# Attention through three ring banks, rotary embedding by copies, silu and the feature split moved in a two-layer hybrid mixer on one core

## The chip, the cores and the metric

The kernel runs on one core of one Trainium2 chip. The metric is the device time of one execution in microseconds (us), lower is better. Arrays are float32; most matrix products are written as three products of float32 halves (high and low parts).

## What is computed

Two layers (`DEPTH = 2`) over 1024 latent and 128 context tokens, 1152 in all, with 1024 features. Each layer normalises the tokens, modulates them, projects them through one combined weight, runs three branches (a gated linear recurrence A, differential attention B, a Fourier mixing C), multiplies each by its own silu gate, projects and merges them under sigmoid gates, and adds an output projection to the residual. For attention, cut to what matters here:

```python
q_b = rms_norm(qb.reshape(B, T, H_B, 2, DH_B), qn_g)      # 4 heads, 2 maps, 64 features
k_b = rms_norm(kb.reshape(B, T, H_B, 2, DH_B), kn_g)
q_b = axial_rope(q_b, rope)                               # latent tokens only: pairs (x1, x2) 16 apart
k_all = concat([axial_rope(k_b, rope), cached context keys])
w = softmax(q1 k1) - lam * softmax(q2 k2)                 # one 128-query block at a time
y_b = rms_norm(w @ v_all, sub_g) * (1 - lam_init) * silu(zb)
```

## The kernel before

Each weight block of 128 output channels is one `project`: three tiles of 384 tokens, each tile 8 x 3 products (high x high, low x high, high x low) into one PSUM bank; `take` hands out banks 0 to 2 in turn, and the reader frees a bank. SyncE loads the blocks in the order of `weight_order` two ahead, GpSimd splits each into high and low parts (L712, L714), TensorE multiplies (L358). The order of the instructions of every engine is written out by hand; semaphores tie them.

In a layer come first the recurrence heads, then `attention(l, h)` for four heads, then the Fourier groups, the merge of the three branches (two products for each of eight feature blocks: a gate G and a branch product Y) and the output projection O. Attention goes over nine positions, `BLOCKS = (0, CTX, 1, ..., 7)`: query blocks of 128, the context block second. At each position and for each of two maps m TensorE forms scores in banks 3 to 5 (L542, L543), VectorE takes the maximum (L1603), ScalarE the exponential (L1048). VectorE forms the weights (L1609 to L1614); TensorE turns them in groups of three 128x128 blocks (`transposed`, L555) through a ring of two banks, 6 and 7, ScalarE copies them (L1055), and TensorE multiplies them with the values (L568), whose result ScalarE reads from the same ring (L1066, L1068).

Between these steps stand projection tiles of the next head (`FIRST_GAP`, one at each position, and `SECOND_GAP`), of q, k, v and of the gate z, in this order: first scores, tile, two groups of turns of the position before, second scores, the third group, a second tile, values of the position before. The preparation of the next head lies there too: `head_sums` (L498) for the norm of q and k, `normed` on VectorE, and the rotary turn, which TensorE does as a product with a constant matrix (`rotated`, L506) whose result VectorE multiplies and adds (`turned`, L1571, L1574). The high and low parts (`high_parts` on ScalarE, `low_parts` on VectorE, L1581 to L1585) are made at the last position. `values_turned` (L515) turns the next head's values at the end of a head, in tile banks; for head 0 it stands behind the first scores. `output_sums`, `output_rstd` and `output_silu` finish the head before at positions 0 and 1; silu needs two table loads.

At the end of a layer ScalarE copies the merged features X to `h_hi` and VectorE forms `h_lo` (L1767) after the last branch product; ScalarE also issues eight loads of the residual, `x_res` (L1264), into the space of the branch features. The residual is added when an output block is ready:

```python
for j in range(KD):
    dve.wait_ge(o_xin, l * 16 * KD + 16 * KD)   # all eight x_res copies
    for t in range(NT):
        ...                                     # X = ps * gate + x_res, frees the tile's bank
```

At the start ScalarE issues the loads of the modulation weights (`ada_group`, 8 of 1 MB), the features X (8 of 576 KB) and the masks; SyncE starts on the weight blocks when the last X has landed. The first layer's features are squared, summed, scaled and modulated feature block by feature block (L1293, L1355, L776, L1359).

Of the kernel before, what the change touches and what calls it, by code (L numbers as in the profile page):

```python
# [19 lines left out]
F32 = mybir.dt.float32  # L20
# [27 lines left out]
IDENT, ONES, HEAD_ONES, ROT = range(4)  # L48
# [22 lines left out]
def weight_order():  # L71
# [3 lines left out]
    qkv = lambda h: [(("B", h, j), False, 20 + 3 * h + j) for j in range(3)]  # L75
    order += [a_block(0, j) for j in range(4)]
# [25 lines left out]
FIRST_GAP = (("q", 0), ("q", 2), ("k", 1), ("k", 2), ("v", 0), ("v", 1), ("v", 2), ("z", 0), ("z", 1))  # L102
SECOND_GAP = {0: ("q", 1), 1: ("k", 0), 8: ("z", 2)}
RING = 34


def mixer_kernel(nc, x_in, w_full, w_half, ada_first, ada_late, cond_rows, params, squares, masks, rope, dft_t, dft_c,
# [12 lines left out]
    off_m = off_c + 4 * 512 + (MASKS + 1) * P  # L120
# [14 lines left out]
    sq_c = at("sq_c", [P, 4, P], F32, off_c)  # L135
    mask = at("mask", [P, MASKS + 1, P], U8, off_c + 4 * 512)
# [17 lines left out]
    ident, ones, head_ones, rot_m = (sq_c[:, i, :] for i in range(4))  # L154
# [90 lines left out]
    with ctx:  # L245
        ps = ctx.enter_context(nc.psum_tensor("ps", [P, 8, 512], F32))

        def sem(name):
# [24 lines left out]
        b_raw_s, b_rs_s, b_qn_s, b_qk, b_vt_s, b_vtok, b_cache_k, b_cache_v, b_kv_out, b_hi, b_lo = (  # L273
            sem(n) for n in ("b_squares", "b_rstd", "b_normed", "b_qk",
                             "b_vt", "b_vtok", "b_cache_k", "b_cache_v", "b_kv_out", "b_hi", "b_lo"))
# [33 lines left out]
        seats = {}  # L309

# [35 lines left out]
        def _(pe):  # L346
            def take(*key):

                bank, nth = len(seats) % NT, len(seats) // NT
                seats[key] = bank, nth + 1  # L350
                if nth:
                    pe.wait_ge(tile_free[bank], nth)
                return bank

# [7 lines left out]
            def tile(l, name, t, kt=KD, hi=h_hi, lo=h_lo):  # L362

                n = place[l, name]
                if t == 0:
                    pe.wait_ge(w_split, n + 2)
                bank = take(l, name, t)
# [60 lines left out]
            def recurrence(l, h):  # L428
                a = l * HEADS + h
                last = h + 1 == HEADS  # L430
                for i, (kind, lev, g) in enumerate(units):
# [49 lines left out]
                    if g == 2:  # L481
# [3 lines left out]
                        if last and point == "ub":  # L485
                            head_sums(l, 0, 1)
                            rotated(l, 0, 0)
                        for name, t in a_gap(h, point):
                            tile(l, name, t)
                        if last and point == "ub":  # L490
                            rotated(l, 0, 1)

            def head_sums(l, h, m):

                for t in range(NT):
                    pe.wait_ge(b_raw_s, (l * HEADS + h) * 6 + (3 * m + t + 1))
                    bank = take(l, "sum", h, m, t)
                    pe.matmul(ps[:, bank, 0:TILE], head_ones, (b_kt if m else b_qt)[:, cols_of(t)],  # L498
                              start=True, stop=True).then_inc(tile_done[bank], 1)

            def rotated(l, h, m):

                pe.wait_ge(b_qn_s, (l * HEADS + h) * 2 + (m + 1))
                for i in range(2):
                    bank = take(l, "rot", h, m, i)
                    pe.matmul(ps[:, bank, :], rot_m, (b_kn if m else b_qn)[:, i * 512:(i + 1) * 512],  # L506
                              start=True, stop=True).then_inc(tile_done[bank], 1)

            def values_turned(l, h):

                pe.wait_ge(b_vt_s, l * HEADS + h + 1)
                for g in range(3):
                    bank = take(l, "vt", h, g)
# [3 lines left out]
                    mm.then_inc(tile_done[bank], 1)  # L517

            def output_sums(l, h):

                for t in range(NT):
                    if t == 0:
                        pe.wait_ge(b_os_s, (l * HEADS + h) * CH + CH)
                    bank = take(l, "osum", h, t)
                    pe.matmul(ps[:, bank, 0:TILE], ones, b_os[:, cols_of(t)],
                              start=True, stop=True).then_inc(tile_done[bank], 1)

            def attention(l, h):
                a = l * HEADS + h
                ring = a * RING  # L530
# [15 lines left out]
                def transposed(pos, g):  # L546
                    nonlocal ring
                    i = BLOCKS[pos]
                    if g == 0:
                        pe.wait_ge(b_w, a * CH + (pos + 1))  # L550
                    if ring > 1:
                        pe.wait_ge(b_ev, ring - 1)
                    for c in range(1 if i == CTX else 3):
                        kt = 3 * g + c
                        mm = pe.transpose(ps[:, 6 + ring % 2, c * P:(c + 1) * P],  # L555
                                          b_e0[pos % 2][:, kt * P:(kt + 1) * P], ident)
                    mm.then_inc(b_tr, 1)
                    ring += 1

                def values(pos):  # L560
                    nonlocal ring
                    i = BLOCKS[pos]
                    if pos == 0:
                        pe.wait_ge(b_vtok, a * 3 + 3)
                        pe.wait_ge(b_cache_v, 16 * a + 16)
                    pe.wait_ge(b_ev, ring)
                    for kt in range(1 if i == CTX else CH):
                        mm = pe.matmul(ps[:, 6 + ring % 2, 0:P], b_v[:, CH if i == CTX else kt, :], b_wt[:, kt, :],  # L568
                                       start=(kt == 0), stop=(kt == CH - 1 or i == CTX))
                    mm.then_inc(b_tr, 1)  # L570
                    ring += 1

                for pos in range(CH):
                    before = 0 if pos == 0 else 1 if BLOCKS[pos - 1] == CTX else 3
# [1335 lines left out]
```

## Time and profile before

| what | value |
|---|---|
| median of three runs | 3163.32 us (3162.22 to 3165.91) |
| the profiled execution's own time | 3163.95 us |
| its span, first to last instruction | 3161.9 us |
| TensorE products busy | 3043.5 us, 96% of the span |
| VectorE, ScalarE, GpSimd busy | 1440.4, 1069.6, 698.7 us |
| mean granted TensorE clock | 0.986 of 2.4 GHz |

The span is 2.05 us shorter than the execution's time. Products overlap in their records: a product of 384 columns is shown with 334 ns, but the next one starts 173 ns after it. An idle gap shown in brackets is the time since the record before ended, which is some 0.16 us after its last column was taken in.

### The profile page before, as it was taken

The page shows a single profiled execution, that of the slowest core. Times are in us where ns is not written, and L with a number is a line of the kernel's source. Part 1 is how long each engine was busy: PE and PEld are TensorE (multiplying, and loading weights), DVE is VectorE, ACT ScalarE, POOL GpSimd, SP SyncE. Part 2 cuts the span into 40 slices and gives each one's busy share as a digit, 9 for nine tenths or more (in the row PEclk, how much of TensorE's full clock was granted, in tenths as well). Part 3 has the DMA queues.
Part 4 walks back from the last instruction along what each step waited for, and adds up shares of the span by engine and source line. Part 5 has one row for each costly group of instructions (what it writes and reads, how often), then busy time and mean ns, then how long its engine had stood idle before and what let it go on. Part 6 is the DMA issues. An engine that isn't in the chain of part 4 may idle for free.

```text
span 3161.9 us, 43735 instructions
## 1 busy us (share of the span) xinstructions
PE 3043.5 (96%) x18336; PEld 2941.6 (93%) x18336; DVE 1440.4 (46%) x1920; ACT 1069.6 (34%) x2036; POOL 698.7 (22%) x404
## 2 busy tenths in 40 slices
PE   7999999999999999999979999999999999999999
PEld 3999988898899999999969999888988999999999
DVE  4655674666542102266247655655655420112331
ACT  5244345656542101111043334456555430101010
POOL 1211111111111233333322111111111122333332
PEclk9999999999999999999999999999999999999999
DMA  5111111000011112154211011100000101212232
GB/s 208 39 31 38 38 49 33 24 23 30 31 71 32 34 42 76 44 160 160 85 44 34 31 38 39 45 31 32 24 30 29 71 28 41 71 47 77 74 111 73
DMA packets 54675, 175.23 MB, mean 55 GB/s; under 512 B 5968, under 2 KB 13136, under 8 KB 52688
## 3 DMA queue, kind: packets, MB, share of 16 engines
q1 hardware_dynamic: 28800, 92.29, 9.6%
q10 hardware_dynamic: 25680, 80.15, 6.9%
q8 instruction: 145, 2.38, 0.3%
q14 instruction: 50, 0.41, 0.0%
HBM read 151.45 MB, written 20.97 MB: 55 GB/s over the span
## 4 chain that ended last, share of the span: by engine, by line
PE 88%; DVE 4%; ACT 3%; ACTq 2%; issue 1%; DVEq 1%; DMA 0%
PE ps L358 66%; PE ps L460 4%; PE ps L568 4%; PE ps L542 2%; PE ps L543 2%; PE ps L555 2%; DVE stat L1603 1%; PE ps L626 1%; PE ps L506 1%; DVE b_qs L1583 1%; PE ps L498 1%; PE ps L628 1%; DVEq L1584 1%; ACT b_eb L1048 1%; PE ps L476 1%
## 5 line engine op out<-in xcount | busy, mean ns | idle before, releaser
L358 PE MATMUL ps<-h_hi,w_hi 128*128 128x384 f32 x3648 | 1242.8, 341 | 35.8 <-DVE h_lo L1396 14.7
L358 PE MATMUL ps<-h_hi,w_lo 128*128 128x384 f32 x3648 | 1226.5, 336 | 0.0
L358 PE MATMUL ps<-h_lo,w_hi 128*128 128x384 f32 x3648 | 1226.2, 336 | 0.0
L712 POOL CAST w_hi<-w_raw 128x1024 fp32r<-128x1024 f32 x200 | 203.4, 1017 | 2421.7 <-PE ps L358 2386.1
L358 PEld LDWEIGHTS ps<-h_hi,w_hi 128*128 128x128 f32 x3648 | 690.8, 189 | 42.6 <-issue 41.4
L358 PEld LDWEIGHTS ps<-h_hi,w_lo 128*128 128x128 f32 x3648 | 691.0, 189 | 1.0 <-issue 0.5
L358 PEld LDWEIGHTS ps<-h_lo,w_hi 128*128 128x128 f32 x3648 | 690.0, 189 | 0.0
L714 POOL TENSOR_TENSOR w_lo<-w_raw,w_hi 128x1024 fp32r<-128x1024 f32 x200 | 495.0, 2475 | 16.0
L1178 ACT ACTIVATE m_g<-ps 128x384 f32<-128x384 f32 x144 | 70.7, 492 | 757.3 <-PE ps L358 735.1
L1603 DVE TENSOR_REDUCE stat<-ps 128x1 f32<-128x1152 f32 (+1 forms) x144 | 177.9, 1235 | 240.7 <-PE ps L543 240.7
L1719 DVE TENSOR_TENSOR m_p<-ps,m_g 128x384 f32<-128x384 f32 x96 | 53.5, 558 | 373.9 <-PE ps L358 373.9
L358 PE MATMUL ps<-y_lo,w_hi 128*128 128x384 f32 x576 | 192.4, 334 | 0.0
L358 PE MATMUL ps<-y_hi,w_hi 128*128 128x384 f32 x576 | 192.4, 334 | 0.0
L358 PE MATMUL ps<-y_hi,w_lo 128*128 128x384 f32 x576 | 192.4, 334 | 0.0
L568 PEld LDWEIGHTS ps<-b_wt,b_v 128*128 128x128 f32 x1168 | 138.9, 192 | 33.5 <-ACT b_wt L1055 24.5
L568 PE MATMUL ps<-b_wt,b_v 128*128 128x128 f32 x1168 | 145.1, 277 | 17.4 <-ACT b_wt L1055 17.4
L542 PE MATMUL ps<-b_kh,b_qs 128*128 128x384 f32 (+1 forms) x400 | 146.6, 366 | 13.8 <-ACT b_eb L1048 9.0
L1719 DVE TENSOR_TENSOR X<-ps,m_g 128x384 f32<-128x384 f32 x48 | 26.8, 558 | 257.5 <-PE ps L358 257.5
L543 PE MATMUL ps<-b_kl,b_qs 128*128 128x384 f32 (+1 forms) x400 | 134.6, 337 | 0.0
L460 PE MATMUL ps<-a_q,a_km 128*128 128x128 f32 x1008 | 132.8, 286 | 0.0
L460 PEld LDWEIGHTS ps<-a_q,a_km 128*128 128x128 f32 x1008 | 127.6, 192 | 2.6 <-ACT a_km L859 1.1
L1048 ACT ACTIVATE b_ea<-ps,stat 128x1152 f32<-128x1152 f32 (+1 forms) x72 | 81.3, 1129 | 143.8 <-DVE stat L1603 143.7
(235 smaller groups left out, 3612.9 us busy)
## 6 DMA issues: line engine op xcount, KB each, us to landing
w_raw<-in_w_full SPq DMA_DIRECT2D x152, 512.0 KB, 3.5
ada_late<-in_ada_late ACTq DMA_DIRECT2D x32, 512.0 KB, 3.6
w_raw<-in_w_half SPq DMA_DIRECT2D x48, 256.0 KB, 2.6
ada_group<-in_ada_first ACTq DMA_DIRECT2D x8, 1024.0 KB, 16.2
X<-in_x_t ACTq DMA_DIRECT2D x8, 576.0 KB, 16.7
y_keep<-a_y ACTq DMA_DIRECT2D x8, 576.0 KB, 3.1
y_keep<-b_z ACTq DMA_DIRECT2D x8, 576.0 KB, 2.8
X<-y_keep ACTq DMA_DIRECT2D x2, 2304.0 KB, 12.0
```

The lines of the kernel that those rows point to most:

```text
L358: mm = pe.matmul(ps[:, bank, 0:TILE], w[:, slot, k, :], r[:, k, cols_of(t)], start=(k == 0 and i == 0), stop=(k == kt - 1 and i == 2))
L460: mm = pe.matmul(o, a_km[lev % 2][:, cs], both_ways(a_q2, c, 1 << lev), start=True, stop=True)
L542: pe.matmul(o, b_qs[:, m, i * P:(i + 1) * P], b_kh[:, m, ks], start=True, stop=False)
L543: mm = pe.matmul(o, b_qs[:, m, i * P:(i + 1) * P], b_kl[:, m, ks], start=False, stop=True)
L555: mm = pe.transpose(ps[:, 6 + ring % 2, c * P:(c + 1) * P], b_e0[pos % 2][:, kt * P:(kt + 1) * P], ident)
L568: mm = pe.matmul(ps[:, 6 + ring % 2, 0:P], b_v[:, CH if i == CTX else kt, :], b_wt[:, kt, :], start=(kt == 0), stop=(kt == CH - 1 or i == ...
L712: pool.tensor_copy(w_hi[:, slot, 0:kt, :], raw).then_inc(w_hi_done, 1)
L714: pool.tensor_tensor(w_lo[:, slot, 0:kt, :], raw, w_hi[:, slot, 0:kt, :].bitcast(F32), ALU.subtract).then_inc(w_split, 1)
L1048: act.activation(dst, src, ACT.Exp, bias=stat[:, pos % 3, m:m + 1], accum_out=stat[:, pos % 3, 2 + m:3 + m]).then_inc(b_exp, 1)
L1178: act.activation(m_g[:, t, :], seen(l, ("G", br, j), t), ACT.Sigmoid)\
L1603: dve.tensor_reduce(stat[:, pos % 3, m:m + 1], src, AX.X if ctx_block else AX.XY, ALU.max, negate=True).then_inc(b_max, 1)
L1719: dve.tensor_tensor(dst, seen(l, name, t), m_g[:, t, :], ALU.mult).then_inc(free(l, name, t), 1)
```

## The change

The rotary turn is done by copies: features are ordered on the host so that the two halves of a pair lie 32 partitions apart, SyncE copies four groups of 32 partitions from the normalised q or k to the place of their norms (`rotate`), issued behind the load of the next head's q block, and VectorE multiplies the copy with signed sines. The constant matrix goes. Turned weights, turned values, output sums and value products all go through one ring of three banks (2, 6, 7); attention's tiles have banks 0 and 1 alone. All three groups of turns stand with the value product behind the second scores, second tiles and head sums behind them; the value product waits for its copies one by one. `values_turned` stands behind the first scores at every head. The order of tiles is q, k, z, v, head sums are spread over four positions, and silu moves from position 1 to position 0. The split of merged features is interleaved with the last branch product. At the start SyncE issues the large loads, with two weight blocks ahead of X, and the order of VectorE's first steps changes.

```diff
-        order += qkv(h + 1) if h + 1 < HEADS else [(("C", g), False, 52 + g) for g in range(3)]
-        order += [(("ZB", h), False, 32 + h)]
+        order += after(h + 1)[:2] + [(("ZB", h), False, 32 + h)] + after(h + 1)[2:]
...
-FIRST_GAP = (("q", 0), ("q", 2), ("k", 1), ("k", 2), ("v", 0), ("v", 1), ("v", 2), ("z", 0), ("z", 1))
-SECOND_GAP = {0: ("q", 1), 1: ("k", 0), 8: ("z", 2)}
-RING = 34
+FIRST_GAP = (("q", 0), ("q", 2), ("k", 0), ("k", 2), ("z", 0), ("z", 1), ("z", 2), ("v", 0), ("v", 1))
+SECOND_GAP = {0: ("q", 1), 2: ("k", 1), 8: ("v", 2)}
+HEAD_SUMS = {1: ((0, 0), (0, 1)), 2: ((0, 2),), 3: ((1, 0), (1, 1)), 4: ((1, 2),)}
+RING = (2, 6, 7)
...
+            def ring_take(*key):
+                n = len(rings)
+                rings[key] = n
+                if n >= len(RING):
+                    pe.wait_ge(b_ev, n - len(RING) + 1)
+                return ring_of(*key)
...
-            def rotated(l, h, m):
-                pe.wait_ge(b_qn_s, (l * HEADS + h) * 2 + (m + 1))
-                for i in range(2):
-                    bank = take(l, "rot", h, m, i)
-                    pe.matmul(ps[:, bank, :], rot_m, (b_kn if m else b_qn)[:, i * 512:(i + 1) * 512],
-                              start=True, stop=True).then_inc(tile_done[bank], 1)
...
                 def values(pos):
-                    pe.wait_ge(b_ev, ring)
+                    bank = ring_take(l, "V", h, pos)
                     for kt in range(1 if i == CTX else CH):
+                        if kt % 3 == 0:
+                            pe.wait_ge(b_ev, rings[l, "T", h, pos, kt // 3] + 1)
...
                 for pos in range(CH):
                     scores(pos, 0)
-                    if pos == 0 and h == 0:
-                        values_turned(l, 0)
+                    if pos == 0:
+                        values_turned(l, h)
                     what, t = FIRST_GAP[pos]
-                    tile(l, gap_block(h, what), t)
+                    tile(l, gap_block(h, what), t, banks=2)
                     if pos == 0 and h:
                         output_sums(l, h - 1)
-                    if before:
-                        transposed(pos - 1, 0)
-                    if before == 3:
-                        transposed(pos - 1, 1)
                     scores(pos, 1)
-                    if before == 3:
-                        transposed(pos - 1, 2)
+                    if pos:
+                        transposed(pos - 1)
+                        values(pos - 1)
                     if pos in SECOND_GAP:
                         what, t = SECOND_GAP[pos]
-                        tile(l, gap_block(h, what), t)
+                        tile(l, gap_block(h, what), t, banks=2)
                     if h + 1 < HEADS:
-                        ...
-                    if before:
-                        values(pos - 1)
+                        for m, t in HEAD_SUMS.get(pos, ()):
+                            head_sum(l, h + 1, m, t, banks=2)
...
+                pe.wait_ge(tile_free[2], uses_of[2])
                 for h in range(HEADS):
                     attention(l, h)
...
         def _(sp):
-            sp.wait_ge(x_in_s[KD - 1], 16)
+            def rotate(l, h, m):
+                src, dst = (b_kn, b_kt) if m else (b_qn, b_qt)
+                sp.wait_ge(b_qn_s, (l * HEADS + h) * 2 + (m + 1))
+                for r in range(0, P, 32):
+                    sp.dma_start(dst[r:r + 32, 0:T_LAT], src[r ^ 32:(r ^ 32) + 32, 0:T_LAT]).then_inc(b_rot[m], 16)
+            group_load(0)
+            group_load(1)
+            weights_load(0, 0)
+            weights_load(0, 1)
+            group_load(2)
+            group_load(3)
+            for k in range(KD):
+                sp.dma_start(X[:, k, :], x_in[:, k, :]).then_inc(x_in_s[k], 16)
+            for i in range(GROUPS, 2 * GROUPS):
+                group_load(i)
+            sp.dma_start(mask_in[:, :, :], masks).then_inc(mask_in_s, 16)
             for l in range(DEPTH):
                 for i, (name, half, index) in enumerate(ORDER):
+                    if l or i >= 2:
+                        weights_load(l, i)
+                    for h in range(HEADS):
+                        if name == (("B", h + 1, 0) if h + 1 < HEADS else ("C", 0)):
+                            rotate(l, h, 0)
+                            rotate(l, h, 1)
...
             # ScalarE, at each position of attention
                     exponentials(pos, 0)
-                    if pos == 1 and h:
-                        output_silu(l, h - 1)
+                    if pos == 0:
+                        read_values(l, h)
...
-                    for g in range(before):
-                        weights_read(pos - 1, g)
+                    if pos:
+                        weights_read(pos - 1)
                     exponentials(pos, 1)
+                    if pos == 0 and h:
+                        output_silu(l, h - 1)
...
+            def merged_high(l, ks):
+                for k in ks:
+                    act.wait_ge(m_done, l * 24 + 16 + k + 1)
+                    act.activation(h_hi[:, k, :], X[:, k, :], ACT.Copy).then_inc(o_hi, 1)
...
+                merged_high(l, range(5))
                 act.wait_ge(*done(l, ("Y", BRANCHES[-1], KD - 1), NT - 1))
                 for k in range(KD):
                     act.dma_start(x_res[:, k, :], x_keep[k] if l else x_in[:, k, :]).then_inc(o_xin, 16)
-                act.wait_ge(m_done, (l + 1) * 24)
-                for k in range(KD):
-                    act.activation(h_hi[:, k, :], X[:, k, :], ACT.Copy).then_inc(o_hi, 1)
+                merged_high(l, range(5, KD))
...
             # VectorE
-            for k in range(2, KD):
-                first_scaled(k)
+            first_scaled(2)
+            first_scaled(3)
+            row_kept(2)
+            first_scaled(4)
+            first_scaled(5)
             first_low(0)
-            row_kept(2)
-            first_low(1)
             row_kept(3)
             modulation(2)
+            first_low(1)
+            first_scaled(6)
             modulation(3)
+            first_scaled(7)
...
             def turned(l, h, m):
                 rs, dst = (b_kt, b_k) if m else (b_qt, b_q)
-                for i in range(2):
-                    cs = slice(i * 512, (i + 1) * 512)
-                    dve.wait_ge(*done(l, "rot", h, m, i))
-                    dve.tensor_tensor(rs[:, cs], ps[:, seat(l, "rot", h, m, i), :], b_rope[:, 1, cs],
-                                      ALU.mult).then_inc(free(l, "rot", h, m, i), 1)
+                dve.wait_ge(b_rot[m], (l * HEADS + h + 1) * 64)
+                dve.tensor_tensor(rs[:, 0:T_LAT], rs[:, 0:T_LAT], b_rope[:, 1, :], ALU.mult)
...
+            def merged_low(l, k):
+                dve.wait_ge(o_hi, l * KD + (k + 1))
+                dve.tensor_tensor(h_lo[:, k, :], X[:, k, :], h_hi[:, k, :].bitcast(F32),
+                                  ALU.subtract).then_inc(o_lo, 1)
             def merge(l, order, br):
...
+                        if order == len(BRANCHES) - 1 and j == KD - 1:
+                            merged_low(l, t)
+                    if order == len(BRANCHES) - 1 and j == KD - 1:
+                        merged_low(l, 3)
```

## Rows read from the trace of the kernel before

**Rows 1.** TensorE's waits: engine, line, releaser: total us, times, longest

```profile
PE ps L568 <- ACT b_wt L1055: 17.4, 30, 0.6
...
PE ps L358 <- DVE h_lo L1767: 13.5, 2, 6.8
...
PE ps L555 <- ACT b_wt L1055: 11.6, 8, 2.2
...
PE ps L542 <- ACT b_eb L1048: 9.0, 8, 2.6
...
PE ps L358 <- ACTq L1012: 5.9, 2, 3.2
```

**Rows 2.** Timeline, all engines, position 6 of head 0: start, us, what

```profile
577.62 0.42 PE L542 MATMUL ps<-b_kh,b_qs 128*128 128x384 f32 x1
...
582.94 0.82 PE L555 MATMUL ps<-sq_c,b_ea 128*128 128x128 f32 x6
...
583.52 0.87 ACT L1055 ACTIVATE b_wt<-ps 128x384 f32<-128x384 f32 x2
...
584.65 0.49 PE L555 MATMUL ps<-sq_c,b_ea 128*128 128x128 f32 x3
...
585.72 2.27 PE L568 MATMUL ps<-b_wt,b_v 128*128 128x128 f32 x18 [0.58 <-ACT b_wt L1055]
586.24 1.22 ACT L1048 ACTIVATE b_eb<-ps,stat 128x1152 f32<-128x1152 f32 x1 [0.58 <-DVE stat L1603]
...
587.75 0.42 PE L542 MATMUL ps<-b_kh,b_qs 128*128 128x384 f32 x1
...
591.51 1.23 ACT L1048 ACTIVATE b_ea<-ps,stat 128x1152 f32<-128x1152 f32 x1 [3.04 <-DVE stat L1603]
```

**Rows 3.** Chain that ended last, 455 to 630 us: start, us, what

```profile
478.77 1.72 PE ps L506 x4
...
500.49 6.97 PE ps L358 x24
...
578.93 4.17 PE ps L358 x24
```

**Rows 4.** Stretches behind waits: us, busy time of engines, PEclk, DMA share, GB/s

```profile
494.00:507.00 13.00, 9.42 (x38) 9.04 (x39) 7.80 (x6) 7.20 (x11) 1.96 (x1) 0.61 0.17 50
860.50:865.50 5.00, 5.00 (x21) 5.00 (x21) 3.58 (x4) 1.37 (x3) 0.00 (x0) 0.66 0.00 0
```

**Rows 5.** Timeline, all engines, from head 0 to head 1

```profile
593.63 0.42 PE L542 MATMUL ps<-b_kh,b_qs 128*128 128x384 f32 x1
...
601.31 3.48 POOL L714 TENSOR_TENSOR w_lo<-w_raw,w_hi 128x1024 fp32r<-128x1024 f32 x1
...
602.58 3.42 DVE L1583 TENSOR_TENSOR b_qs<-b_q,b_qs 64x1152 fp32r<-64x1152 f32 x1
...
608.43 1.35 DVE L1583 TENSOR_TENSOR b_qs<-b_q,b_qs 64x1152 fp32r<-64x1152 f32 x1
...
614.56 0.63 PE L542 MATMUL ps<-b_kh,b_qs 128*128 128x384 f32 x1
```

**Rows 6.** Line L1264, x_res issues: ns min/median/max, first and last start; landing

```profile
L1264 ACTq DMA_DIRECT2D x_res<-in_x_t x8: 334/487/576, 1486.2 to 1489.7; - x8
...
DMA to landing us min/median/max: 3.6/8.2/12.7
```

**Rows 7.** Timeline around the first layer's output projection

```profile
1486.17 0.56 DVE L1719 TENSOR_TENSOR m_p<-ps,m_g 128x384 f32<-128x384 f32 x1 [1.53 <-PE ps L358]
...
1506.91 0.41 PE L358 MATMUL ps<-h_hi,w_hi 128*128 128x384 f32 x1
```

**Rows 8.** DMA in 40 slices of 0 to 40 us: GB/s

```profile
GB/s 0 42 210 421 408 393 401 410 442 410 426 410 451 383 416 420 401 415 419 419 415 433 396 415 418 453 400 423 434 434 410 426 406 410 438 381 411 413 270 25
```

**Rows 9.** Timeline of the start, VectorE and ScalarE

```profile
24.91 8.61 DVE L1293 TENSOR_TENSOR n_acc<-n_acc,n_sq 128x1152 f32<-128x1152 f32 x6
...
58.94 1.25 ACT L776 ACTIVATE X<-X,mod,amul 128x1024 f32<-128x1024 f32 x1 [2.01 <-DVE amul L1351]
```

More of the change, by code:

```diff
@@ L45 @@
 KEYS = T
-IDENT, ONES, HEAD_ONES, ROT = range(4)
+IDENT, ONES, HEAD_ONES = range(3)
+SQUARES = 3
 MASKS = 5
@@ L75, in weight_order @@
     qkv = lambda h: [(("B", h, j), False, 20 + 3 * h + j) for j in range(3)]
+    after = lambda h: qkv(h) if h < HEADS else [(("C", g), False, 52 + g) for g in range(3)]
     order += [a_block(0, j) for j in range(4)]
@@ L152, in mixer_kernel @@
     SPACE = nc.sbuf_usable_end - off_s
-    ident, ones, head_ones, rot_m = (sq_c[:, i, :] for i in range(4))
+    ident, ones, head_ones = (sq_c[:, i, :] for i in range(SQUARES))
     off_b = off_s + EXT
@@ L309, in mixer_kernel, with ring_of @@
         seats = {}
+        uses_of, latest = [0] * NT, [0, 1, 2]
+        rings = {}
+        def ring_of(*key):
+            return RING[rings[key] % len(RING)]
         def done(*key):
@@ L346, in _, with take @@
         def _(pe):
[L347 to L352, printed above, removed]
-                return bank
+            def take(*key, banks=NT):
+                bank = next(b for b in latest if b < banks)
+                latest.remove(bank)
+                latest.append(bank)
+                if uses_of[bank]:
+                    pe.wait_ge(tile_free[bank], uses_of[bank])
+                uses_of[bank] += 1
+                seats[key] = bank, uses_of[bank]
+                return bank
+            def ring_take(*key):
[4 more added lines that the diff above has]
+                return ring_of(*key)
             def product(slot, bank, t, k, kt, hi, lo):
@@ L360, in product, with tile @@
                 return mm
-            def tile(l, name, t, kt=KD, hi=h_hi, lo=h_lo):
+            def tile(l, name, t, kt=KD, hi=h_hi, lo=h_lo, banks=NT):
                 n = place[l, name]
@@ L366, in tile @@
                     pe.wait_ge(w_split, n + 2)
-                bank = take(l, name, t)
+                bank = take(l, name, t, banks=banks)
                 for k in range(kt):
@@ L512, in values_turned @@
                 for g in range(3):
-                    bank = take(l, "vt", h, g)
+                    bank = ring_take(l, "vt", h, g)
                     for c in range(3 * g, 3 * g + 3):
@@ L523, in output_sums @@
                         pe.wait_ge(b_os_s, (l * HEADS + h) * CH + CH)
-                    bank = take(l, "osum", h, t)
+                    bank = ring_take(l, "osum", h, t)
                     pe.matmul(ps[:, bank, 0:TILE], ones, b_os[:, cols_of(t)],
-                              start=True, stop=True).then_inc(tile_done[bank], 1)
+                              start=True, stop=True).then_inc(b_tr, 1)
             def attention(l, h):
                 a = l * HEADS + h
-                ring = a * RING
                 def scores(pos, m):
@@ L544, in scores, with transposed @@
                     mm.then_inc(b_sc, 1)
-                def transposed(pos, g):
-                    nonlocal ring
+                def transposed(pos):
                     i = BLOCKS[pos]
[L549 to L558, printed above, removed]
+                    pe.wait_ge(b_w, a * CH + (pos + 1))
+                    for g in range(1 if i == CTX else 3):
+                        bank = ring_take(l, "T", h, pos, g)
+                        for c in range(1 if i == CTX else 3):
+                            kt = 3 * g + c
+                            mm = pe.transpose(ps[:, bank, c * P:(c + 1) * P],
+                                              b_e0[pos % 2][:, kt * P:(kt + 1) * P], ident)
+                        mm.then_inc(b_tr, 1)
@@ L721, in _ @@
             act.dma_start(sq_c[:, :, :], squares).then_inc(const_in, 16)
-            def group_load(i):
-                q, half = i // 2, slice(4 * (i % 2), 4 * (i % 2) + 4)
-                act.dma_start(groups[q][:, half, :], ada_first[q, :, half, :]).then_inc(group_in[i], 16)
-            for i in range(GROUPS):
-                group_load(i)
             act.wait_ge(const_in, 32)
@@ L1762, in _ @@
                 merge(l, 2, BRANCHES[2])
[L1765 to L1768 removed]
+                for k in range(4, KD):
+                    merged_low(l, k)
                 for j in range(KD):
```

195 lines of the change are left out of this document (82 added, 113 removed).

## The prediction

> **What bounds the kernel now.** I read the page's busy shares first (TensorE is busy nearly all the span, so time can only come from its own work, from its idle stretches and from its clock), then who TensorE waits for, then one attention position in order of time, then the chain of waits at the start of attention, and last the two ends of a layer.
>
> [rows 1] is the list of waits. Three belong to attention: the value product L568 waits 30 times for ScalarE's copies of the turned weights (17.4 us), the turns L555 wait for the same copies (11.6 us), the scores L542 for the exponential (9.0 us). L358 waits twice at the first head (5.9 us). The rest lies at the start, at the second layer's normalisation, and where a layer's merged features are split.
>
> [rows 2] is a plain position of attention, from one first score product (577.62) to the next (587.75): 10.13 us. Scores and one projection tile take 5.32 us (to 582.94), then two groups of turns, the second scores, the third group at 584.65. The value product starts only at 585.72, 1.07 us later, after a turn and its copy; it lasts 2.03 us. Beside it runs a loop that TensorE sees only through the scores: exponential at 586.24, then VectorE's weights and next maximum, next exponential at 591.51: 5.27 us from one to the other.
>
> [rows 3] prices three things: a stage of two rotary products is 1.72 us of TensorE; a tile is 4.17 us; the same 24 products after the first head's wait take 6.97 us. [rows 4] shows why: there the granted clock was 0.61 in the mean, so part of the stretch ran at 1.2 GHz after TensorE had stood idle. A later wait shows 0.66.
>
> **The change, part by part** (every sum against the profiled execution, 3163.95 us, 2.05 us above its span; the median is 0.63 us below it).
>
> *Rotary products leave TensorE.* Two inputs, four heads, two layers are 16 stages of 1.72 us: 27.5 us off. Four of them stand ahead of the first head's attention in the chain itself [rows 3], the other twelve between scores. In their place SyncE issues 4 copies of 128 KB per input. In attention query and key are normalised at positions 3 and 5 and used one position later, some 10 us; the longest landing of a larger copy of 576 KB is 12.7 us, for eight in a row [rows 6], so I take them as hidden. While it waits, SyncE holds the next weight load, which is not read until the next head's third position: also hidden.
>
> *The first head's turned values move to the ring.* The tile behind them no longer waits for a tile bank: 5.9 us, and twice 6.97 - 4.17 = 2.8 us of slow clock, 11.5 us. Two things give back: attention now waits for bank 2 (one copy, about 0.5 us, in the first layer alone, where bank 2 holds the last value tile), and a shorter wait before the first scores stays and may hold the clock down (the same 1.3 us as below, in each layer). Net 8.4; bounds 6 and 11.5.
>
> *All nine turns behind the second scores, three banks.* The value product can start after the first group and its copy: by [rows 2] 1.07 us after the turns begin. Six turns take 0.82 and three 0.49, so one more costs 0.11 and the nine issue for 0.98. The wait seen now, 0.58 and the tail of a product, 0.74 in all, becomes 0.1 to 0.2: 0.57 us at each of the 24 of the 30 waits that lie inside heads, 13.7 us. About 20 positions whose gap was covered by other products now pay 0.17: -3.4. Net 10.3.
>
> *Silu at position 0, second tiles behind the values.* The waits of L555 for copies behind silu and of L542 for the exponential sum to 20.6 us in 16 places [rows 1], 23.2 with the tail of 0.16 that each record hides. What stays is a turn, its copy and a one-product value at the context block, about 0.8 us a head: -6.4. Net 16.8; at four of these waits the clock fell (one is shown in [rows 4]); 5 us at 0.66 lose at most 1.7, I take 1.3 each: 5.2.
>
> *Head changes.* From the last block's second scores to the next head's second scores TensorE takes 20.93 us now (593.63 to 614.56) [rows 5]. The turned values move behind the new head's first scores; the ring that the output sums take is then free only when ScalarE, after its first exponential, has copied them (about 2 us). I put the stretch between 19.9 (all covered) and 22.5 us (the low parts meet GpSimd as today) and take 21.8: 0.9 us lost at six changes, -5.5.
>
> *Merged features split under the last product.* Now the output projection stands idle for up to 6.8 us after the last product [rows 1]; after it only the last multiplication is in the way: 1486.17 + 0.56, so about 1486.8, and it ends 72 products x 0.173 = 12.5 us later, at 1499.3. But its three banks are freed by the residual, which needs all eight x_res copies: issued from 1486.2 to 1489.7, the last landing 12.7 us later, 1502.4 [rows 6]. Today the products end at 1506.9 [rows 7] and do not see it; then they will. The second projection would start at about 1503.1, not 1506.9: 3.8 us, and since the clock was low behind the wait it replaces and behind the first head's, I count half of that one's 2.8 us, 1.4, as lost again. Net 2.4 a layer, 5.0; bounds 3 and 15 (the copies not late).
>
> *Start.* [rows 8]: the transfers are the limit, at some 410 GB/s for 35 us. Two weight blocks, 1 MB, now come ahead of the features and cost these 2.6 us. Against that the sums of squares, which end at 33.5 [rows 9], no longer start late behind ScalarE's issuing; they would follow the landings and end between 31.8 and 33.5. The fifth scaling waits 2.01 us for the modulation; its new order frees most of it. I take 1.7 + 2.1 = 3.8; bounds 0 and 7.
>
> *VectorE's rotary product* read PSUM and now reads two SBUF operands. [rows 5]: an L1583 that runs beside GpSimd's split took 3.42 us, alone 1.35. I take 2 us in all; bounds 0 and 25 (below). The Trainium skill, page "SBUF — State Buffer", section "SBUF: two separate sides", says that an operation of VectorE with two SBUF inputs and a GpSimd operation exclude each other for a whole instruction, which speaks against this edit; the trace's 3.42 us agrees in kind. By that rule the sum would lose a GpSimd instruction at every meeting; by the rows alone most products fall where GpSimd is idle.
>
> **Sum:** 27.5 + 8.4 + 10.3 + 16.8 + 5.2 - 5.5 + 5.0 + 3.8 - 2 = 69.5 us. 3163.95 - 69.5 - 0.63 gives **3094 us**.
>
> **Rivals.**
> *The loop becomes the bound (20%).* In the new order the third copy ends about 1.7 us after the turns begin (1.07 for the first; two take 0.87 [rows 2], so each further one adds some 0.4, less the hand-over). Then come exponential, weights, maximum, exponential (5.27) and 1.22 with some 0.1 of hand-over until scores can go: 8.3 us. TensorE gets there at 3.1 + 5.32 = 8.4. For: the margin is 0.1 us, and the cover between the two scores shrinks by two groups of turns. Against: today the maximum is ready with no wait. With 0.5 us more in the loop, positions 3 to 7 of eight heads cost 20 us: 3114.
> *The x_res copies don't hold the output projection (10%).* If they land early enough the split gives 15 instead of 5: 3084. Against: the 12.7 us [rows 6].
> *GpSimd holds the rotary products (8%).* Twelve in attention, each 3.42 - 1.35 = 2.07 late with the maximum behind it: 25 us in place of 2, 3117. Against: the split takes about 3.5 us and starts when a block's last tile ends, at positions 1, 3, 6 and 8; the products run at 4 and 6.
> *TensorE's freed time turns into waits (7%).* If the positions are paced by the other engines throughout, the twelve stages in heads (20.6) and the 10.3 give nothing: 3125.
> *Slower (3%).* SyncE stands on a normalised key, and the next head's key block comes late. It would have to be missed by some 10 us at each of eight heads to undo the rest (3174); that needs the key normalised some 50 us late, since the block has from position 5 to the next head's position 2, six positions of 10 us [rows 2].
>
> **The numbers.** My forecast 3094 holds 52%, its own range 3076 to 3109. The range 3068 to 3120 takes in the loop, the early copies and GpSimd's hold, and leaves out the last two rivals and the tails. About 0.2%, 6 us, is what a measurement of this kernel can tell from no change. All cases but the last are faster: 96%; 1% same; 3% slower.
>
> **What the profile will show.** No L506; rotary copies landing before VectorE's product asks. Value products with waits near 0.1 us, positions 5 to 7 of a head near 9.6 us. No 3 us wait at the first head. A wait of L358 near the output projection's second block, released by VectorE after x_res. I am wrong if scores wait at every position, if head changes take over 23 us, or if weights are late.

## The result, and the profile after

The changed kernel takes 3085.41 us (median of 4 runs, 3083.95 to 3086.50) against 3164.33 for the kernel before: ratio 0.9751, 95% interval 0.9734 to 0.9768, faster. The forecast was 3094, its range 3068 to 3120. The profiled execution has a span of 3083.2 us (before 3161.9) at a mean granted clock of 0.994 (before 0.986): 78.7 us less.

Where they went is read from the starts of the same instruction in both timelines (us):

| TensorE starts | before | after | gained in the stretch | forecast |
|---|---|---|---|---|
| second weight block | 73.62 | 69.21 | 4.4 | 3.8 |
| first scores, layer 1 and 2 | 494.37, 2054.76 | 487.29, 2010.05 | 2.7 + 4.0 | 6.4 (four stages, less the wait for bank 2) |
| first tile behind attention | 930.23, 2493.77 | 894.97, 2418.08 | 28.2 + 31.0 | 54.3 (20.6 + 8.9 + 10.3 + 16.8 + 5.2 - 5.5 - 2) |
| output projection, second block | 1506.91, 3070.26 | 1467.91, 2991.54 | 3.7 + 3.0 | 5.0 |
| second layer's first product | 1612.01 | 1571.33 | 1.7 | 0 |

The list of TensorE's waits, which answers to [rows 1] (line, releaser: total us, times, longest):

```profile
PE ps L578 <- ACT b_wt L1072: 7.3, 20, 0.5
...
PE ps L538 <- ACTq L1032: 4.9, 6, 1.1
PE ps L528 <- ACT b_o L1080: 4.1, 6, 0.7
PE ps L379 <- DVE X L1792: 3.6, 2, 2.1
PE ps L554 <- ACT b_vt L984: 3.0, 1, 3.0
...
PE ps L379 <- DVE m_p L1731: 2.4, 2, 1.2
PE ps L379 <- DVE h_lo L1719: 2.2, 2, 1.1
```

The 38 waits of [rows 1] for copies in attention are 20 short ones. Gone are the waits for the exponential and for the tile at the first head; of the 13.5 us for the split 4.6 are left (m_p L1731, which was in the forecast, and h_lo L1719, which was not). New are two at each head change (the turned values L528 wait for the ring, the output sums L538 for the copies of the values) and one for the residual (L1792). The wait L554 stands ahead of the first layer's first scores, for the copy that empties bank 2. Before, the scores waited there too, but for another releaser:

```profile
PE ps L542 <- ACTq L868: 2.1, 1, 2.1
```

The timeline of the same position 6 of head 0, which answers to [rows 2]:

```profile
552.36 0.42 PE L554 MATMUL ps<-b_kh,b_qs 128*128 128x384 f32 x1
...
556.01 1.21 DVE L1579 TENSOR_TENSOR b_kt<-b_kt,b_rope 128x1024 f32<-128x1024 f32 x1
556.13 1.22 ACT L1065 ACTIVATE b_ea<-ps,stat 128x1152 f32<-128x1152 f32 x1 [3.05 <-DVE stat L1610]
...
557.67 0.33 PE L554 MATMUL ps<-b_kh,b_qs 128*128 128x384 f32 x1
...
558.71 1.14 PE L565 MATMUL ps<-sq_c,b_ea 128*128 128x128 f32 x9
...
559.24 1.25 ACT L1072 ACTIVATE b_wt<-ps 128x384 f32<-128x384 f32 x3 [0.88 <-PE ps L565]
...
559.87 2.25 PE L578 MATMUL ps<-b_wt,b_v 128*128 128x128 f32 x18
560.31 0.34 ACTq L1105 DMA_DIRECT2D out_k_new<-b_kn  x1
560.37 1.23 ACT L1065 ACTIVATE b_eb<-ps,stat 128x1152 f32<-128x1152 f32 x1
...
561.88 0.42 PE L554 MATMUL ps<-b_kh,b_qs 128*128 128x384 f32 x1
```

9.52 us instead of 10.13. The nine turns issue in one go, the value product follows 1.16 us after their start with no wait, and the copies of the groups end (560.49) after it has begun. VectorE's product with the rotated key (556.01) starts right behind the maximum.

The rotary copies (line L702, then the product L1579: ns min/median/max, first and last start):

```profile
L702 SPq DMA_DIRECT2D b_qt<-b_qn x32: 512/591/598, 447.2 to 2258.0; - x32
L702 SPq DMA_DIRECT2D b_kt<-b_kn x32: 507/592/1349, 468.5 to 2279.3; - x32
...
DMA to landing us min/median/max: 2.2/2.3/3.1
```

```profile
L1579 DVE TENSOR_TENSOR b_qt<-b_qt,b_rope x8: 1215/1215/1226, 464.5 to 2265.5; 128x1024 f32<-128x1024 f32 x8
...
  DMA b_kt<-b_kn: 5.5, 2
```

They land within 3.1 us of their issue. VectorE waits for them twice, for the first head's key in each layer (5.5 us in all). Its product takes 1.21 to 1.23 us every time.

From head 0's last second scores to head 1's, the head change of [rows 5], 21.74 us:

```profile
576.71 0.33 PE L554 MATMUL ps<-b_kh,b_qs 128*128 128x384 f32 x1
...
598.45 0.63 PE L554 MATMUL ps<-b_kh,b_qs 128*128 128x384 f32 x1
```

The first layer's output projection, which answers to [rows 7]:

```profile
1451.60 5.19 DVE L1719 TENSOR_TENSOR h_lo<-X,h_hi 128x1152 fp32r<-128x1152 f32 x2
...
1452.04 0.41 PE L379 MATMUL ps<-h_hi,w_hi 128*128 128x384 f32 x1 [1.21 <-DVE m_p L1731]
...
1452.18 3.38 POOL L738 TENSOR_TENSOR w_lo<-w_raw,w_hi 128x1024 fp32r<-128x1024 f32 x1
...
1459.87 0.41 PE L379 MATMUL ps<-h_hi,w_hi 128*128 128x384 f32 x1 [1.12 <-DVE h_lo L1719]
...
1467.15 1.79 DVE L1792 SCALAR_TENSOR_TENSOR X<-ps,mod,x_res 128x384 f32<-128x384 f32 x4 [3.62 <-DMA x_res<-in_x_t]
...
1467.91 0.41 PE L379 MATMUL ps<-h_hi,w_hi 128*128 128x384 f32 x1 [1.56 <-DVE X L1792]
```

VectorE stands 3.62 us for x_res, and TensorE behind it 1.56. The granted clock by stretch (us, busy time of five engines, PEclk, DMA share, GB/s), first the kernel after at the first head and at the output projection, then the kernel before at the output projection:

```profile
487.00:500.00 13.00, 12.71 (x67) 12.65 (x68) 9.28 (x9) 8.51 (x13) 0.99 (x1) 0.87 0.30 101
1452.00:1470.00 18.00, 15.27 (x84) 14.45 (x85) 13.11 (x11) 3.99 (x4) 6.91 (x4) 1.00 0.75 293
```

```profile
1486.00:1510.00 24.00, 17.18 (x91) 16.95 (x91) 14.29 (x14) 9.71 (x9) 7.08 (x4) 0.86 0.64 248
```

The start, VectorE's sums of squares, which answers to [rows 9]; they end at 30.11 instead of 33.52:

```profile
22.95 7.16 DVE L1299 TENSOR_TENSOR n_acc<-n_acc,n_sq 128x1152 f32<-128x1152 f32 x5
```

### The profile page after: what moved, and what is told of

Same layout as the page of the kernel before. It is cut to its first block, busy times and chain, and to the rows that moved or that the text cites. A ratio compares the mean times of both kernels' runs of the same rounds, so it can differ in the third digit from the quotient of the medians.

```text
span 3083.2 us, 43695 instructions
## 1 busy us (share of the span) xinstructions
PE 3003.7 (97%) x18272; PEld 2917.0 (95%) x18272; DVE 1436.7 (47%) x1904; ACT 1066.7 (35%) x2036; POOL 684.6 (22%) x404
## 4 chain that ended last, share of the span: by engine, by line
PE 92%; DVE 2%; ACT 2%; DMA 2%; ACTq 1%; issue 1%; DVEq 0%; SPq 0%
PE ps L379 69%; PE ps L578 4%; PE ps L481 4%; PE ps L555 2%; PE ps L554 2%; PE ps L565 2%; PE ps L515 1%; PE ps L618 1%; PE ps L620 1%; PE ps L538 1%; DVE b_kl L1588 1%; DMA X<-in_x_t 1%; PE ps L497 1%; PE ps L629 1%; PE ps L479 1%; PE ps L628 1%
## 5 line engine op out<-in xcount | busy, mean ns | idle before, releaser
L738 POOL TENSOR_TENSOR w_lo<-w_raw,w_hi 128x1024 fp32r<-128x1024 f32 x200 | 482.4, 2412 | 16.0
L1731 DVE TENSOR_TENSOR m_p<-ps,m_g 128x384 f32<-128x384 f32 x96 | 53.5, 557 | 369.2 <-PE ps L379 369.2
L554 PE MATMUL ps<-b_kh,b_qs 128*128 128x384 f32 (+1 forms) x400 | 145.4, 364 | 5.1 <-ACT b_vt L984 3.0
L1731 DVE TENSOR_TENSOR X<-ps,m_g 128x384 f32<-128x384 f32 x48 | 26.8, 557 | 257.3 <-PE ps L379 257.3
```

The source lines that it names most:

```text
L554: pe.matmul(o, b_qs[:, m, i * P:(i + 1) * P], b_kh[:, m, ks], start=True, stop=False)
L738: pool.tensor_tensor(w_lo[:, slot, 0:kt, :], raw, w_hi[:, slot, 0:kt, :].bitcast(F32), ALU.subtract).then_inc(w_split, 1)
L1731: dve.tensor_tensor(dst, seen(l, name, t), m_g[:, t, :], ALU.mult).then_inc(free(l, name, t), 1)
```

## The experiments

Theory: TensorE sets the pace in attention, with the loop of exponential, weights and maximum just behind it, and each part gains because TensorE has less to do or wait for. Rivals stand with each run. Times are medians; the kernel before took 3163.35 to 3164.33 beside them, and the changed kernel, run again, 3085.98.

> The changed kernel itself, as a measure for the three that follow on the same chip: 3085 us.

Measured 3085.98, ratio 0.9757 (0.9744 to 0.9771).

**The rotary products, from both sides.** Alone on the kernel before:

```diff
-                        if pos == 3:
-                            rotated(l, h + 1, 0)
...
-                        if pos == 5:
-                            rotated(l, h + 1, 1)
...
+                            rotate(l, h, 0)
+                            rotate(l, h, 1)
```

> The kernel before with one part of the change: the rotary products leave TensorE, SyncE's copies and the sorted columns take their place; turns, ring, silu, split and start stay as before. My theory, the forecast's term as it stands: 16 stages of 1.72 us, -27.5 us, about 3136. Rival (a stage between the turns and the value product also covered the wait for the turned weights' copy, so that alone it is worth only the difference between position 5 and position 6 of the kernel before, 10.99 - 10.09 = 0.9 us, at 12 places, and 1.72 at the four ahead of the first head): 12 x 0.9 + 6.9 = 17.7 us, about 3146. Third (the freed time is all waits): -7, 3156.

Measured 3145.78, ratio 0.9943 (0.9929 to 0.9956): -18.0 us, near the rival's 17.7. Positions 3 and 5 of six heads went from 10.99 to 10.16 and 10.12, not down by 1.72: 10.2 us in all, near the rival's 10.8. The wait of the value products (17.4 us, 30 times in [rows 1]) grew:

```profile
PE ps L558 <- ACT b_wt L1054: 24.3, 42, 0.6
```

Twelve more waits: each stage had covered one. That the total agrees too is partly luck. By the starts, as in the table above, the four stages ahead of the first heads gave 5.6 us, not 6.9; around the output projections 3.2 were lost; and 6.5 came from four positions whose instructions the edit left alone: position 3 of the last heads (11.68 and 11.72 before, 10.14 here) and position 1 of two heads in the second layer (15.30 and 15.56 before, 13.73 here). There the clock differs and not the work. At position 3 of the first layer's last head the wait is the same, but behind it the granted clock is 0.85 in the kernel before and 1.00 here:

```profile
860.29 0.44 PE L542 MATMUL ps<-b_kh,b_qs 128*128 128x384 f32 x1 [2.57 <-ACT b_eb L1048]
860.29:871.97 11.68, 11.10 (x63) 10.80 (x64) 5.24 (x7) 4.65 (x10) 3.40 (x2) 0.85 0.01 1
```

```profile
852.39 0.44 PE L532 MATMUL ps<-b_kh,b_qs 128*128 128x384 f32 x1 [2.58 <-ACT b_eb L1047]
852.36:862.50 10.14, 9.53 (x63) 9.23 (x64) 5.24 (x7) 4.69 (x10) 3.40 (x2) 1.00 0.01 2
```

Then the products put back into the changed kernel (SyncE's copies go, VectorE reads the products from PSUM again):

```diff
+                        if pos in (3, 5):
+                            rotated(l, h + 1, pos // 2 - 1)
```

> The changed kernel with the rotary products back on TensorE (two products of 512 columns for each input and head, at the ends of positions 3 and 5, and ahead of the first head), all else as changed. My theory: TensorE sets the pace of these positions, so each stage costs its own time again: 12 x 1.72 in heads = 20.6 us and 4 x 1.72 ahead of the first head = 6.9 us, 27.5 in all: about 3113 us. Rival (the freed time had turned into waits on the other engines): only the four ahead of the first head count, +7 us, about 3092.

Measured 3150.49, ratio 0.9963 (0.9950 to 0.9976): +64.5 us, beyond both. TensorE's waits show why:

```profile
PE ps L379 <- DVE b_qt L1592: 12.8, 6, 2.1
PE ps L379 <- DVE b_kt L1592: 12.3, 6, 2.0
```

The two products take both tile banks that attention has left, and the next tile waits until VectorE has read them a position later: 25.1 us. Positions 3 and 5 grow by 2.1 and 1.4 us for the stages, 4 and 6 by 2.5 and 2.6 behind these waits: 52 us in six heads. Ahead of the first heads the four stages cost 6.3 us. So in this order of work the tiles can do with two banks, and the ring have three, because the rotary products hold none; no run tried them at another place.

**The ring.**

```diff
-RING = (2, 6, 7)
+RING = (6, 7)
```

> The changed kernel with a ring of two banks (6 and 7) in place of three, turns still all behind the second scores. My theory: with two banks the third group of turns waits for the first group's copy and the value product for the second's; it starts about 0.5 us later at each of the 8 positions of a head whose blocks have nine turns, 64 in all, +32 us, and more where the copies then reach the second exponential late: 3110 to 3125. Rival (the order of the turns alone made the gain, the third bank is idle room): under +5 us, 3085 to 3090.

Measured 3152.59, ratio 0.9970 (0.9960 to 0.9979): +66.6 us, twice the theory's. Waits:

```profile
PE ps L528 <- ACTq L1032: 33.2, 8, 4.9
PE ps L565 <- ACT b_wt L1072: 19.4, 64, 0.5
...
PE ps L528 <- ACT b_o L1080: 6.3, 6, 1.1
```

The third group of turns waits 64 times, as expected, but for 0.3 us each. The rest stands at the head's start: the third group of turned values now needs a bank that ScalarE frees only behind the first exponential, up to 4.9 us. The clock falls behind these waits too: position 0 of heads 1 and 2 of the first layer takes 22.55 and 22.18 us at a granted clock of 0.85, where the changed kernel takes 15.33 and 15.34 at 1.00. The third bank is worth more there than in the plain positions.

**Silu.**

```diff
+                    if pos == 1 and h:
+                        output_silu(l, h - 1)
...
                     exponentials(pos, 1)
-                    if pos == 0 and h:
-                        output_silu(l, h - 1)
```

> The changed kernel with the silu of the previous head's gate (and the table load behind it) back between the first exponential and the first tile's read of position 1, where it was before. My theory (silu ahead of the copies of the turned weights was what held TensorE at position 1): position 1 of six heads goes from 9.2 to about 13 us, position 0 gives back some 2: about +2 at each of six heads, +12 us, 3097. Rival (the second tiles behind the value products made that gain, and silu's place is worth nothing): 3085 to 3088.

Measured 3099.37, ratio 0.9804 (0.9789 to 0.9819): +13.4 us, the theory's total, but not by its parts. Position 1 went from 9.20 to 11.05 (12.72 in one head; in the last heads from 7.88 to 9.20), not to 13, and position 0 did not get shorter (15.34). The value product waits:

```profile
PE ps L578 <- ACT b_wt L1072: 18.0, 22, 2.3
```

**The loop's margin.** One more VectorE instruction, whose result nobody reads, between those that combine the weights:

```diff
+                    dve.tensor_reduce(stat[:, e, 7:8], b_e1[:, 0:min(wide, 384)], AX.X, ALU.max)
```

> The changed kernel with one more VectorE instruction between the two that combine the weights at every position: a maximum over 384 columns whose result nobody reads, some 0.4 us. My theory (as forecast, the loop of exponential, weights, maximum, exponential is within 0.1 us of TensorE's own work): positions 3 to 7 of eight heads grow by about 0.3 us each, 12 us, and the rest by some 4 more: 3097 to 3102. Rival (the loop has half a microsecond and more to spare): under +3 us, 3085 to 3088.

Measured 3100.85, ratio 0.9808 (0.9793 to 0.9822): +14.9 us, as the theory. The added instruction (ns min/median/max, first and last start) and first, second and next first scores of position 6 in head 1:

```profile
L1620 DVE TENSOR_REDUCE stat<-b_eb x72: 268/546/549, 500.4 to 2428.1; 128x1 f32<-128x384 f32 x64, 128x1 f32<-128x128 f32 x8
```

```profile
657.99 0.42 PE L554 MATMUL ps<-b_kh,b_qs 128*128 128x384 f32 x1
...
663.59 0.45 PE L554 MATMUL ps<-b_kh,b_qs 128*128 128x384 f32 x1
...
667.91 0.42 PE L554 MATMUL ps<-b_kh,b_qs 128*128 128x384 f32 x1
```

9.92 us instead of 9.52: of 0.55 us put into the loop, 0.40 came through, so the margin is some 0.15 us. It came through at positions 6 to 8, at position 0 of the next head, and from 4 on in the last head of a layer; positions 1 to 5 of the other heads did not grow. So the total is the theory's, while the places are only in part its positions 3 to 7.

**The start and the split, alone on the kernel before**, with the changed kernel's code for each:

> The kernel before with one part of the change: SyncE issues all loads at the start, two weight blocks ahead of the features, and VectorE takes scalings, rows and low parts in the new order. My theory: the first products' end moves by what the changed kernel shows, -4.4 us: about 3159. Rival (1 MB ahead of the features costs the 2.6 us that the bandwidth says and only the order of VectorE gains, 2): within 1 us of before.

Measured 3157.10, ratio 0.9981 (0.9973 to 0.9990): -6.6 us; the second weight block starts 4.25 us earlier. In its trace 3.0 us more were gained in the second layer's attention, where position 1 of two heads had lasted 15.30 and 15.56 us in the profiled execution before (13.73 in the others) and lasts 13.72 and 14.04 here, with the same instructions. That is the clock, not the edit: in the first of the two TensorE waits 1.84 us at the same place in both traces, and the granted clock of the position is 0.89 before and 1.00 here.

> The kernel before with one part of the change: the merged features are split under the last products. My theory: the output projection starts 5.5 us earlier in each layer, its second block then waits for the residual's x_res copies and gives back about 2; -3.4 and -3.0 as in the changed kernel, -6.4 us, about 3157. Rival (the copies are no limit, the second block waits only for VectorE): -11, 3152. Second rival (the clock falls again behind the shorter wait, as forecast): -5, 3158.

Measured 3152.53, ratio 0.9967 (0.9955 to 0.9979): -11.2 us. In its trace the two layers' second blocks start 3.7 and 4.2 us earlier against the stretch before, 7.9; 2.65 more lie in the second layer's attention, at those two positions again, and 1.7 between the layers. So the total is near the rival's, while the mechanism is the theory's: the block waits 1.56 us for VectorE, and VectorE 3.65 us for x_res, as in the changed kernel.

**VectorE's order at the start**, put back to the old one:

```diff
-            first_scaled(2)
-            first_scaled(3)
-            row_kept(2)
-            first_scaled(4)
...
+            for k in range(2, KD):
+                first_scaled(k)
+            first_low(0)
+            row_kept(2)
```

> The changed kernel with VectorE's old order at the start (all scalings behind the second modulation, then the low parts and rows), SyncE still issuing all loads. My theory: the forecast's 2.1 us for the fifth scaling's wait come back: +2 us, 3087.5. Rival (the landings set the start, the order is free): 0, 3085.5.

Measured 3088.38, ratio 0.9763 (0.9750 to 0.9776): +3.0 us on the first measurement of the changed kernel, +2.4 on the one above; the second weight block starts at 71.08 instead of 69.21, 1.9 later.

**The residual by block.**

```diff
+        o_xin = [sem(f"o_x_in{k}") for k in range(KD)]
...
-                    act.dma_start(x_res[:, k, :], x_keep[k] if l else x_in[:, k, :]).then_inc(o_xin, 16)
+                    act.dma_start(x_res[:, k, :], x_keep[k] if l else x_in[:, k, :]).then_inc(o_xin[k], 16)
...
-                    dve.wait_ge(o_xin, l * 16 * KD + 16 * KD)
+                    dve.wait_ge(o_xin[j], l * 16 + 16)
```

> The changed kernel with a semaphore for each of the eight x_res copies, so that the residual of block j waits for its own copy alone. My theory (the last landing holds the output projection's second block, 2.1 us a layer of which VectorE's own reading needs some 0.6): -3 us, 3082.5. Rival (VectorE's low parts and reading hold it): 0, 3085.5.

Measured 3081.92 (3080.78 to 3083.08), ratio 0.9743 (0.9730 to 0.9757): 4.1 us below the changed kernel run beside it (3085.03 to 3088.57), and the fastest version here. VectorE's residual now waits for the product, not for a copy:

```profile
1464.67 1.79 DVE L1793 SCALAR_TENSOR_TENSOR X<-ps,mod,x_res 128x384 f32<-128x384 f32 x4 [1.90 <-PE ps L380]
```

**The head change in another order.** First tile ahead of the turned values, output sums behind the second tile:

```diff
-                    if pos == 0:
-                        values_turned(l, h)
                     what, t = FIRST_GAP[pos]
                     tile(l, gap_block(h, what), t, banks=2)
-                    if pos == 0 and h:
-                        output_sums(l, h - 1)
+                    if pos == 0:
+                        values_turned(l, h)
                     scores(pos, 1)
...
+                    if pos == 0 and h:
+                        output_sums(l, h - 1)
```

> The changed kernel with another order at a head's first position: first scores, first tile, the turned values, second scores, second tile, then the output sums of the head before (ScalarE reads them after silu). My theory: the two waits of the head change, 4.1 us for the ring (L528) and 4.9 us for the copies of the values (L538), are filled with the tile: -9 us, 3076. Rival (the head change is held by the loop from the first scores to the second, or VectorE's output now comes late for position 1): 0 or slower, 3085 to 3090.

Measured 3091.12, ratio 0.9773 (0.9759 to 0.9786): 5.1 us slower than the changed kernel, so the theory fell. The two waits went, but position 0 gained 0.7 us and position 1 lost 2.2, where the scores now wait for an exponential behind the sums' work on ScalarE:

```profile
PE ps L554 <- ACT b_ea L1065: 10.8, 12, 1.6
```

> The changed kernel with both: the late output sums and the residual gated by block. If both theories hold, -12 us, 3073.5; if only the residual's, 3082.5; if only the sums', 3076.

Measured 3089.47, ratio 0.9767 (0.9754 to 0.9780): the residual's gain, by 1.7 us here, on top of that loss.

## Why the prediction was right, point by point

**Rotary products (27.5).** Ahead of the first head 6.7 us were gained of 6.4 forecast, copies hidden but for one wait of VectorE in each layer that costs TensorE nothing. The 20.6 in the heads fit the changed schedule: put back there, the stages lengthen positions 3 and 5 by 2.1 and 1.4 us, 21 in six heads. On the schedule before they do not: alone the twelve stages give 10.2, because each also covered a wait for a copy. What was missing came only with the new order of the turns, so this term and the next do not stand by themselves.

**First head (8.4).** Position 0 went from 18.12 and 17.86 us to 13.12 and 13.10, 9.8 in two layers, against 8.9 without the 0.5 for bank 2. A wait before the first scores stayed, 3.0 us in the first layer (L554) and 2.2 in the second, and the clock is 0.87 behind it, as forecast. The first layer's is the wait for bank 2: it grew by 0.9 from 2.1, where 0.5 was taken.

**Turns, banks, silu (10.3, 16.8, 5.2).** Positions 5 to 7 take 9.71, 9.52 and 9.51 us where 9.6 was written. Silu's place alone is worth 13.4. The whole of attention, 59.2 against 54.3, was 4.9 under-estimated: 0.9 at the first head, 2 on VectorE's product (below), 1.3 at the four positions where the clock had fallen (6.5 lost there, 5.2 taken), less 0.5 at the head changes, and some 1.2 that no run tells apart. The 5.2 rest on those clock losses of the kernel before, and three of the runs above (rotary_alone, start_alone, split_alone) lack two or four of them with the same waits: that they came back in full is in part luck.

**Head changes (-5.5).** 21.74 us measured (22.1 once), 21.8 forecast.

**VectorE's rotary product (-2).** No cost: 1.215 us each, at most 1.226, where two reads of PSUM had taken 0.68 us each. None met a split on GpSimd.

**Merge (5.0).** 6.7. The x_res copies hold the second block as forecast: 15.1 us from the projection's start to VectorE's release, 15.6 forecast. (Two layers of 2.4 are 4.8; the sum took 5.0.) The step that failed is the clock: 2.8 us were counted as lost behind a wait, and the row shows 1.00. Against it a wait of 1.1 us in each layer for a late low part was not foreseen.

**Start (3.8).** 4.4. The sums ended 3.4 us earlier (forecast 0 to 1.7). The two weight blocks ahead of the features cost less than the 2.6 us forecast: the last feature block landed only 0.7 us later (28.87 instead of 28.15), as the first load had landed 2.4 us earlier (6.90 instead of 9.26). The order of VectorE gave 1.9 (2.1).

**Rivals.** The loop did not become the bound, but its margin is as small as written (0.15 us, 0.1 forecast): half a microsecond more in it costs 15. The time lies near the rival without x_res (3084), yet x_res did hold; its removal gives another 4.1, so the split without it is worth some 11 us, not that rival's 15. The forecast was 8.6 us too high; by the starts, 9.2: 4.9 in attention, 1.7 at the merge, 1.7 between the layers and 0.9 at the start and ahead of the first head. The 1.7 between the layers are the clock: from the output projection's second block to the second layer's first product the kernels with the split take 103.4 us in some runs (the changed kernel, split_alone) and 105.1 in others (order_undone), as before. In the last 16 us of that stretch the granted clock is 0.85 in the first two, 0.75 in order_undone and 0.68 before.

**How far the cause is shown.** Run alone, the rotary copies, the split and the start give 18.0 + 11.2 + 6.6 = 35.8 us, where 36.3 were forecast for them, but in other shares (27.5, 5.0, 3.8), and some of each is the clock. The other 43 us, turns, ring, silu and the head's start, were tested only by undoing the ring and silu. The order of the tiles, the spread of the head sums and the new place of the turned values were not run singly.

## What to carry to other kernels

A part's worth is that of the schedule it is put in: the same rotary products were worth 18 us on the old schedule and cost 64 on the new one, 25 of them waits for the banks they hold. Work that stands between a producer's copy and its reader covers a wait; before it is removed, see what else could cover it. When a new wait names a transfer, see whether its reader needs all of it: a semaphore for each block gave 4 us more.

## What was not expected of the hardware

VectorE's two subtractions L1719 at 1451.60 took 5.19 us together, where one alone takes 1.34 (at 1449.87), and GpSimd's split L738 beside them 3.38 us instead of 2.4. That is as if each ran only when the other had ended: 1451.60 + 1.34 + 2.4 + 1.34 = 1456.7, measured 1456.79. The Trainium skill, page "SBUF — State Buffer", section "SBUF: two separate sides", states this: a VectorE operation with two inputs in SBUF and a GpSimd operation that reads SBUF hold the shared port in turn, each for its whole instruction; the trace agrees. The cost came not at the rotary product, where it was looked for, but at the low parts: 1.12 us of TensorE in each layer.

Waits of 1.1 to 1.6 us at the output projection left the granted clock at 1.00; the wait of up to 6.8 us there before had brought the stretch to 0.86. In attention the same wait did either: behind 2.57 us the granted clock of the position was 0.85 in one kernel and 1.00 in another, behind 1.84 us 0.89 and 1.00. A part of a few microseconds that a run gains or loses can be this, and only the clock rows of both traces tell.
